# Third mixer of a three-block transformer kernel: latent products as whole jobs before the gate products, head norms regrouped over the engines, attention groups spaced out over the gate blocks

## The reference, cut to what matters

```python
proj = h @ w_in                      # q_lat 192, kv_lat 128, k_rope 32, fq/fk/fv 512 each, f_logit 8, g_mla 1024, g_fox 1024
q  = rms_norm(q_lat) @ w_qb          # 8 heads x (64 nope + 32 rope)
kv = rms_norm(kv_lat) @ w_kvb        # 8 heads x (64 nope + 64 value)
# MLA:  heads normed, rope on q and on the shared k_rope, causal softmax attention
# FoX:  fq, fk normed by head; logits + (c[t] - c[s]), c = cumsum(log_sigmoid(f_logit + b_f))
mixed = sigmoid(g_mla + b0) * (y_mla @ w_branch_mla) + sigmoid(g_fox + b1) * (y_fox @ w_branch_fox)
x = x + mixed @ w_o
```

## Time and profile before

| what | value |
|---|---|
| time, median of 3 runs | 1527.27 us (1527.05 to 1529.64) |
| profiled execution, its own time | 1527.37 us |
| its span | 1525.6 us |
| PE busy | 1489.3 us (98%) |
| DVE, ACT, POOL busy | 876.5, 713.4, 84.6 us |
| mixer three | about 1146.6 to 1334 us of the span |

### The profile page before, as it was taken

How to read it: one execution, slowest core, us unless ns; L and a number is a source line. 1 busy time by engine, 2 the same in 40 slices (tenths; PEclk the granted TensorE clock), 3 DMA queues, 4 the chain that set the end, 5 groups by cost and what they waited for, 6 DMA issues and landing times.

```text
span 1525.6 us, 17528 instructions
## 1 busy us (share of the span) xinstructions
PE 1489.3 (98%) x7341; PEld 1251.1 (82%) x7341; DVE 876.5 (57%) x1051; ACT 713.4 (47%) x846; POOL 84.6 (6%) x101
## 2 busy tenths in 40 slices
PE   8999999999999999999799999999999889999999
PEld 6888888888888888888688888888888768888887
DVE  5464456555445654559765554754547786765453
ACT  6444345544344443344554444543436656454342
POOL 0000012000000000006000000000000440000000
PEclk9999999999999999999999999999999989999999
DMA  8546473455466554644455466554656352555462
GB/s 312 174 146 212 136 257 101 140 181 191 138 217 197 193 182 149 207 147 152 136 180 193 135 210 206 181 192 140 218 169 208 119 166 83 193 177 188 141 225 69
DMA packets 143077, 265.71 MB, mean 174 GB/s; under 512 B 7022, under 2 KB 23878, under 8 KB 142742
## 3 DMA queue, kind: packets, MB, share of 16 engines
q1 hardware_dynamic: 141894, 260.23, 52.0%
q0 software_dynamic: 1104, 4.35, 0.8%
...
...
## 4 chain that ended last, share of the span: by engine, by line
PE 88%; DVE 8%; ACT 2%; POOL 1%; issue 1%; DMA 0%; POOLq 0%; SPq 0%; DVEq 0%; ACTq 0%
PE ps L531 27%; PE ps L533 27%; PE ps L532 27%; DVE wlo L1446 2%; PE ps L560 2%; PE ps L543 1%; ACT whi L1071 1%; PE ps L908 1%; POOL m_qf L2064 0%; PE ps L712 0%; PE ps L656 0%; DVE d_i L1773 0%; DVE X L1501 0%; PE ps L622 0%; DVE d_m L1769 0%
## 5 line engine op out<-in xcount | busy, mean ns | idle before, releaser
L1446 DVE TENSOR_TENSOR wlo<-raw,whi 128x2048 fp32r<-128x2048 f32 (+4 forms) x280 | 570.6, 2042 | 456.4 <-ACT whi L1071 455.4
L1071 ACT CAST whi<-raw 128x2048 fp32r<-128x2048 f32 (+4 forms) x280 | 475.5, 1701 | 484.8 <-PE ps L533 477.1
L531 PE MATMUL ps<-whi,xt_hi 128*128 128x512 f32 (+3 forms) x1472 | 553.3, 376 | 5.6 <-DVE xt_lo L1460 3.0
L533 PE MATMUL ps<-whi,xt_lo 128*128 128x512 f32 (+3 forms) x1472 | 546.8, 371 | 0.0
L532 PE MATMUL ps<-wlo,xt_hi 128*128 128x512 f32 (+3 forms) x1472 | 546.4, 371 | 0.0
L531 PEld LDWEIGHTS ps<-whi,xt_hi 128*128 128x128 f32 x1472 | 278.3, 189 | 55.4 <-DVE xt_lo L1460 4.7
L533 PEld LDWEIGHTS ps<-whi,xt_lo 128*128 128x128 f32 x1472 | 278.2, 189 | 48.0
L532 PEld LDWEIGHTS ps<-wlo,xt_hi 128*128 128x128 f32 x1472 | 278.4, 189 | 45.5
L1093 ACT ACTIVATE junk<-X 128x512 f32<-128x512 f32 x40 | 25.3, 632 | 58.5 <-DVE X L1501 55.0
L531 PE MATMUL ps<-whi,yt_hi 128*128 128x512 f32 (+3 forms) x108 | 43.4, 402 | 8.1 <-DVE wlo L1446 6.9
L533 PE MATMUL ps<-whi,yt_lo 128*128 128x512 f32 (+3 forms) x108 | 42.0, 389 | 0.0
...
## 6 DMA issues: line engine op xcount, KB each, us to landing
...
```

What stands on the lines that cost most here:

```text
L531: e.matmul(o, h, hi_w, start=i == 0 and j == 0, stop=False)
L533: t = e.matmul(o, l, hi_w, start=False, stop=end and j == nk - 1)
L1071: e.copy(whi[0:n, v % SPLIT, c], raw[0:n, v % RAW, c]).then_inc(s_hi.mark(*[(v, j) for j in js]), 1)
L1446: e.tensor_tensor(wlo[0:n, v % SPLIT, c], raw[0:n, v % RAW, c], whi[0:n, v % SPLIT, c].bitcast(F32), ALU.subtract).then_inc(s_lo.mark(*[(v ...
```

## The change

Both parts of w_qb become one job of one block with 768 columns, whose product fills two PSUM pairs, and both halves of w_kvb one job with 1024 columns (block 9). The plan of the mixer is then 26 blocks: 7 is w_qb, 8 fv, 9 w_kvb, 10 to 17 the gates. Both latent products come before the first gate block. The norms of fq and fk share one computation of factors, and POOL multiplies both; DVE multiplies q; the key's rope moves from DVE to POOL. POOL's 16 decay operations become two of 16x256 and two of 16x2048. The second copy of each transposed softmax (P1) moves from DVE to ACT (`flips`). The steps of the two attention kinds are spread over the gate blocks in a new order on PE, ACT and DVE. The diff, indentation cut, lines of removed order left out where the printed functions show them:

```diff
@@ Job, plan, buffers
+self.parts = [(name if c == 0 else f"{name}_{c}", c, min(512, self.width - c)) for c in range(0, self.width, 512)]
...
                                + [(1896 + 512 * i, 512) for i in range(4)], XT, ("xt", "c1"))
-qb = [Job(f"qb{i}", T["mla_w_qb_2"][0], [(0, 2, (128, 64))], [c], YT, ("yt", "lat")) for i, c in enumerate([(0, 512), (512, 256)])]
-kvb = [Job(f"kvb{i}", T["mla_w_kvb_2"][0], [(0, 1, 128)], [(512 * i, 512)], YT, ("yt", "lat"), 2) for i in range(2)]
+qb = Job("qb", T["mla_w_qb_2"][0], [(0, 2, (128, 64))], [(0, 768)], YT, ("yt", "lat"))
...
-    + together(lat, fq) + both(fk) + [(fv, 0), (qb[0], 0), (fv, 1), (qb[1], 0)]
-    + [(gate2[0], 0), (kvb[0], 0), (gate2[0], 1), (kvb[1], 0)] + both(gate2[1]) + both(gate2[2]) + both(gate2[3])
+    + together(lat, fq) + both(fk) + [(fv, 0), (qb, 0), (fv, 1), (kvb, 0)]
+    + both(gate2[0]) + both(gate2[1]) + both(gate2[2]) + both(gate2[3])
...
+r24f = sb("m_rf", [128, 32], F32, sc)
...
-kr_room = [sb("m_kr1", [128, 32], F32, sc), sb("m_kr2", [128, 32], F32, sc)]
...
+kr_room = [mat.P1[:, 0, 0:32], mat.P1[:, 0, 32:64]]
...
@@ TensorE: steps()
+        for pair, (part, c0, w) in zip(pairs, job.parts):
+            hi_w, lo_w = (b[0:n, v % SPLIT, j * wd + c0:j * wd + c0 + w] for b in (whi, wlo))
+            o = pair.ap[:, tt, 0:w]
+            e.matmul(o, h, hi_w, start=i == 0 and j == 0, stop=False)
+            e.matmul(o, h, lo_w, start=False, stop=False)
+            t = e.matmul(o, l, hi_w, start=False, stop=end and j == nk - 1)
+            if j == nk - 1:
+                t.then_inc(s_mm.mark(*([(part, tt)] if end else []), *([(v, tt)] if c0 + w == wd else [])), 1)
...
@@ TensorE: mla()
     def fox_turn(g):
-        q.wait_ge(*s_pool["hn", "fq"])
+        q.wait_ge(*s_pool["hn", "fk"])
...
-        q.wait_ge(*s_dve["hn", "fk"])
...
+    steps(qb, 0)
+    give(qb.parts[0][0], s_act["qf"])
+    give(qb.parts[1][0], s_act["qf"])
     steps(fv, 1)
     give(fv.name, s_act["fv"])
...
+    steps(kvb, 0)
+    give(kvb.parts[0][0], s_act["kv"])
+    give(kvb.parts[1][0], s_act["kv"])
     fox_turn(0)
...
+    steps(gate2[0], 0, 0, 2)
+    fox_scores(0)
+    steps(gate2[0], 0, 2)
     fox_turn(1)
...
+    steps(gate2[0], 1, 0, 2)
     fox_scores(1)
...
+    steps(gate2[0], 1, 2)
+    give(gate2[0].name, s_dve["gate", 0])
+    steps(gate2[1], 0, 0, 2)
     probabilities(mat, ("f", 0), 0)
...
+    steps(gate2[1], 0, 2)
     fox_values(0)
...
+    rope_key_turn()
+    steps(gate2[1], 1, 0, 1)
+    mla_turn(0)
+    steps(gate2[1], 1, 1, 3)
+    mla_scores(0)
+    steps(gate2[1], 1, 3)
+    give(gate2[1].name, s_dve["gate", 1])
     probabilities(mat, ("f", 1), 1)
...
+    steps(gate2[2], 0, 0, 1)
+    mla_turn(1)
+    steps(gate2[2], 0, 1, 3)
     fox_values(1)
...
+    mla_scores(1)
     steps(gate2[2], 0, 3)
...
+    steps(gate2[2], 1, 0, 3)
+    probabilities(mat, ("m", 0), 0)
+    steps(gate2[2], 1, 3)
     give(gate2[2].name, s_dve["gate", 2])
...
+    steps(gate2[3], 0, 0, 1)
     mla_values(0)
+    steps(gate2[3], 0, 1)
     probabilities(mat, ("m", 1), 1)
...
+    steps(gate2[3], 1, 0, 2)
+    mla_values(1)
+    steps(gate2[3], 1, 2)
     give(gate2[3].name, s_dve["gate", 3])
...
@@ ScalarE: mla()
+    def second_copy(g):
+        e.copy(mat.P1[:, :, :], Pair(("m_", "p", g, 1)).flat[:, 0:512].rearrange("p (h t) -> p h t", h=4)).then_inc(s_act.mark(("m_", "P1", g)), 1)
+
+    def flips(g, before=None):
+        probabilities(mat, g, before)
+        q.wait_ge(*s_turn["m_", "p", g, 1])
+        second_copy(g)
...
                          accum_out=s24[:, 2 * i + tt:2 * i + tt + 1]).then_inc(s_act.mark(("latsq", tt, i)), 1)
     unit()
+    norm_squares("fq")
     turned("latt", YT, 0, lambda i: gain(("ql", "ql2", "kvl")[i]), (128, 64, 128))
     unit()
-    norm_squares("fq")
     scaled("fk", lambda tt: FK[:, tt, :], fk, RS)
+    norm_squares("fk")
     unit()
...
+    for part, c0, w in qb.parts:
+        q.wait_ge(*s_mm[part, 1])
+        for tt in range(2):
+            t = e.mul(QF[:, tt, c0:c0 + w], Pair(part).ap[:, tt, 0:w], r_lat[:, tt:tt + 1])
+    t.then_inc(s_act.mark("qf"), 1)
+    unit()
+    norm_squares("q")
     scaled("fv", lambda tt: FV[:, tt, :], fv, RS)
     unit()
+    for part, c0, w in kvb.parts:
+        q.wait_ge(*s_mm[part, 1])
+        for tt in range(2):
+            t = e.mul(KVF[:, tt, c0:c0 + w], Pair(part).ap[:, tt, 0:w], r_lat[:, 2 + tt:3 + tt])
+    t.then_inc(s_act.mark("kv"), 1)
     fox_turn(0)
...
+    norm_squares("k")
     unit()
     fox_turn(1)
+    unit()
     softmax(mat, ("f", 0), 0)
+    unit()
     softmax(mat, ("f", 1), 1)
...
+    flips(("f", 0))
     turned(("m_", "v", ("f", 0)), YT, 4, None, (128,) * 2)
...
     q.wait_ge(*s_turn["m_", "s", ("f", 1), 0])
     q.wait_ge(*s_turn["krt"])
     e.copy(mKT[64:96, :, :], bc(Pair("krt").ap[64:96, 0, 0:256], 1, 8)).then_inc(s_act.mark("krt"), 1)
+    unit()
     mla_turn(0)
+    flips(("f", 1), ("f", 0))
+    unit()
     mla_turn(1)
     softmax(mat, ("m", 0), 0)
+    turned(("m_", "v", ("f", 1)), YT, 6, None, (128,) * 2)
+    unit()
     softmax(mat, ("m", 1), 1)
...
+    flips(("m", 0), ("f", 1))
     unit()
     turned(("m_", "v", ("m", 0)), YT, 0, None, (128,) * 2)
...
+    flips(("m", 1), ("m", 0))
+    unit()
...
@@ VectorE: mla()
...
+    def norm_sums(name, c0):
+        for i, x in enumerate(norm_views[name]):
             n = x.shape[2]
             src = norm_room[i % 2][:, 0:8 * n].rearrange("p (h n) -> p h n", h=8)
             q.wait_ge(*s_act["hnsq", name, i])
             q.wait_ge(*norm_done[0])
...
+            e.tensor_reduce(s24[:, c0 + 8 * i:c0 + 8 * i + 8], src, AX, ALU.add).then_inc(s_dve.mark(("hns", name, i)), 1)
+
+    def norm_factors(names, dst, widths):
         after_mine()
...
+        k = 8 * len(widths)
+        rsqrt(s24, k, [(8 * i, 8, 1.0 / n) for i, n in enumerate(widths)], dst[:, 0:k], ("hnr", names))
...
+    unit()
     q.wait_ge(*s_act["latsq", 1, 2])
     rsqrt(s24, 6, [(0, 2, 1.0 / 192), (2, 2, 1.0 / 128), (4, 2, 1.0 / 32)], r_lat[:, :], ("rs", "lat"))
...
+    norm_sums("fq", 0)
     turned("latt", ("yt", "lat"), YT, 0, lambda i: gain(("ql", "ql2", "kvl")[i]), (128, 64, 128))
     q.wait_ge(*s_turn["ft"])
     e.tensor_scalar(C[64:80, 0, :], Pair("ft").ap[64:80, 1, 0:256], G[64:80, gcols["bff"]:gcols["bff"] + 1], None,
                     ALU.add).then_inc(s_dve.mark("fz"), 1)
     unit()
...
+    after_mine()
+    e.scalar_tensor_tensor(C[64:80, 1, :], C[64:80, 0, :], -1.0, C[64:80, 0, :], ALU.mult, ALU.max).then_inc(s_dve.mark("fabs"), 1)
+    after_mine()
+    e.tensor_scalar(C[64:80, 0, :], C[64:80, 0, :], 0.0, 1.0, ALU.min, ALU.mult).then_inc(s_dve.mark(), 1)
+    norm_sums("fk", 16)
+    norm_factors("f", r24f, (64,) * 4)
+    unit()
+    q.wait_ge(*s_act["fln"])
+    after_mine()
+    e.scalar_tensor_tensor(C[64:80, 0, :], C[64:80, 1, :], -1.0, C[64:80, 0, :], ALU.mult, ALU.add).then_inc(s_dve.mark(), 1)
     q.wait_ge(*s_pool["c_ones"])
     after_mine()
     e.tensor_tensor_scan(C[64:80, 1, :], C[64:80, 2, :], C[64:80, 0, :], 0.0, ALU.mult, ALU.add).then_inc(s_dve.mark("c"), 1)
...
+    unit()
+    unit()
+    norm_sums("q", 0)
+    norm_factors("q", r24, (64, 64, 32, 32))
+    after_mine()
+    for i, x in enumerate(norm_views["q"]):
+        e.tensor_tensor(x, x, r24[:, 8 * i:8 * i + 8].unsqueeze(2).broadcast_to([128, 8, x.shape[2]]),
+                        ALU.mult).then_inc(s_dve.mark(*([("hn", "q")] if i == 3 else [])), 1)
+    unit()
+    norm_sums("k", 0)
+    norm_factors("k", r24, (64, 64))
     unit()
     logits(mat, ("f", 0), 0, 1.0, causal)
+    unit()
+    normalise(mat, ("f", 0), 0)
     logits(mat, ("f", 1), 1, 1.0, causal, ("fxk", 1))
...
+    unit()
+    gate(0)
     normalise(mat, ("f", 1), 1)
...
     turned(("m_", "v", ("f", 0)), ("yt", "fox"), YT, 4, None, (128,) * 2)
...
+    unit()
+    logits(mat, ("m", 0), 0, 96.0 ** -0.5, causal, ("m_", "p", ("f", 0), 1))
+    unit()
+    gate(1)
+    normalise(mat, ("m", 0), 0)
     turned(("m_", "v", ("f", 1)), ("yt", "fox"), YT, 6, None, (128,) * 2)
...
     logits(mat, ("m", 1), 1, 96.0 ** -0.5, causal, ("m_", "p", ("f", 1), 1))
...
+    unit()
     normalise(mat, ("m", 1), 1)
     unit()
     gate(2)
...
     turned(("m_", "v", ("m", 0)), ("yt", "mla"), YT, 0, None, (128,) * 2)
...
+    unit()
+    turned(("m_", "v", ("m", 1)), ("yt", "mla"), YT, 2, None, (128,) * 2)
     gate(3)
     unit()
...
@@ GpSimd: mla()
...
+    def scale_heads(names, rows_):
+        views = [v for n in names for v in norm_views[n]]
         for i, x in enumerate(views):
             after_mine()
...
+            t = e.tensor_tensor(x, x, rows_[:, 8 * i:8 * i + 8].unsqueeze(2).broadcast_to([128, 8, x.shape[2]]), ALU.mult)
+            t.then_inc(s_pool.mark(*([("hn", names[-1])] if i == len(views) - 1 else [])), 1)
+
+    q.wait_ge(*s_dve["rs", "lat"])
+    q.wait_ge(*s_gate["all"])
+    for tt in range(2):
+        kr = KR[:, tt, 64:96]
+        after_mine()
```

(77 more changed lines are left out.)

97 lines of the change are left out of this document (7 added, 90 removed).

## The result

The changed kernel takes 1534.35 us, median of 6 runs (1533.26 to 1536.39); the kernel before, run beside it, 1529.61 (1527.05 to 1530.4). The ratio is 1.0036, interval [1.0023, 1.0049]: slower, by some 3.5 to 7.5 us. The profiled spans say the same, 1531.5 against 1525.6 us. The forecast was slower, 1539.

The account below looks back on a forecast made before the run. PE was taken as the bound. Waits of 24.8 us against 11.8 gave +13.0, clock 0, small gaps -1.0: net +12.0 on the profiled execution's 1527.4, so 1539 us, range 1522 to 1546.

Parts of the forecast that it names:

- the two large waits: PE waits 10.4 us in the keys' half of fox_turn(1), for DVE's logits, and 5.4 in mla_turn(1), for gate(1).
- the clock's cost: PE's slow spells behind waits: 5.6 us behind the gaps of 10.4 and 5.4, against 5.7 before, so 0 net.
- Step 1: Block 8 on DVE: PE, done with w_qb, waits 1.7 us for its split.
- Step 5: Pair of gate 1: PE waits 5.4 us in mla_turn(1), as gate(1) on DVE stands behind the split of block 16.
- The small waits: fox_values(0) and mla_scores(0) wait some 0.4 us each for ACT, 0.8 in the sum.
- faster: Rival, chance 0.10: with short holds, the pair in mla_turn(1) is also read in time; 1519 us.
- Short holds: Rival, chance 0.17: POOL's long additions hold DVE only briefly, the 10.4 us wait in fox_turn(1) goes; 1529 us.
- step 4: DVE held up to 9.2 us by POOL's two additions; first FoX logits late, PE waits 10.4 us in fox_turn(1).
- Steps 2 and 3: PE waits 3.1 us at gate 0 for ACT's kv scaling, then 3.4 at the FoX scores for POOL's decay rows.
- the 1.0 us: Small gaps at PE's switches between products and transposes, estimated to vanish in the waits: -1.0 us in the sum.

Follow-up runs that it names:

- gate first: Changed kernel with gate(1) moved ahead of the split of block 16 on DVE; 1527.86 us, ratio 1.0003 to the kernel before.
- rows cut: Changed kernel with POOL's two 16x2048 additions cut to one head of eight, the other rows zero; 1532.03 us, ratio 1.0023 to the kernel before.
- small rows: Changed kernel with the 16 decay operations of 16x256 of before back on POOL; 1534.77 us, ratio 1.0043 to the kernel before.
- logits first: Changed kernel with the first FoX logits on DVE directly behind block 11, before block 12 and the k norm; 1532.7 us, ratio 1.0029.
- both: Changed kernel with gate(1) before block 16 and the first FoX logits before the k norm; 1526.48 us, ratio 0.9989 to the kernel before.
- late key norm: As both, with the k norm behind the second logits and gate(0), first normalisation behind the second logits; 1522.91 us (0.9970), again 1523.6 (0.9974).
- Block 8 first: Changed kernel with the split of block 8 ahead of the shared factors of fq and fk on DVE; 1535.38 us, ratio 1.0058.
- four rooms: Changed kernel with four work buffers instead of two for ACT's squares of the head norms; 1534.4 us, ratio 1.0050 to the kernel before.

## Why the prediction was right, and where it was too high

**Right.** PE's work and busy time unchanged; DVE the late engine; the two large waits in the two places and with the two releasers named; the clock's cost the same as before (mixer busy 125.9 in both). Step 1: 1.5 us for 1.7. Step 5: 5.2 for 5.4, and gate first shows that its mechanism is the one given, the gate behind the split of block 16. The small waits: 0.8 for 0.8. The *faster* rival needed `gate(1)` within 1.8 us of the probabilities, and it ended at 1260.8, 6.5 us behind the end of their last transposes. *Short holds* falls as well: holds of 2.2 and 3.3 us can be read directly, and rows cut has their price.

**Too high by 6 us on the profiled execution, 4.7 by the median; first term: step 4, the size of additions and holds.** I had bounded an addition between 4.2 and 5.2 us, and it took 3.60, below the lower bound. The holds were put at the full length of both, 9.2 us; they were 5.5. Of these 3.7 us, 2.0 are the additions' own length, and most of the rest comes from the first one, which had begun 1.25 us before DVE came to an operation that it holds. From the q factors to their last instruction DVE took 8.7 us where the sum had 13.3, and although it began them 1.2 late, the logits began at 1220.8 and not at 1224.4. That is 3.6 us of the 6.

**Second term: where the clock's cost lies.** Behind the two large waits I had 5.6 us. Behind the first, PE's starts from 1222.05 to 1226.22 lose 1.9 us against the same instructions at the full clock, behind the second 1.4, together 3.3. The rest of the low clock, 2.7 us from 1190 to 1197, came ahead of the logits, where PE would have waited anyway. By both corrections the sum is 12.0 - 3.6 - 2.3 = 6.1; the mixer time says 6.2. That they meet to 0.1 us is luck: the 1.0 us below, which the sum had taken off, is not in this reckoning, and step 5's 0.2 neither.

**Steps 2 and 3: two single waits wrong, without effect.** The ring's wait was 1.5 (forecast 3.1), and there was none for the decay rows (3.4). The ring's was short by the clock: gate 0 began 32.3 us after the first mark in the changed kernel as in rows cut, small rows, logits first, gate first, both and late key norm, where the wait is 2.7 us, near the forecast; in the changed kernel the longer spell at the lower clock (from 1189.3 to 1195.4) filled 1.2 of them. Both waits stand ahead of the logits on PE, while DVE sets when those come: had they been right, the 9.0 us would have been smaller by as much. Block 8 first and four rooms confirm it. The rows had a margin of 0.6 us (ready at 1206.05, scores at 1206.64), and small rows turned it into a wait of 2.7. The 1.0 us that I let vanish in the gaps at each switch did not vanish: idle time is 17.96 us, all of it in the table of waits.

**Still open.** What decides whether PE runs at the lower clock behind a wait, and for how long. The same instructions behind nearly the same wait do both. Behind the 5.2 us before `mla_turn(1)` the transposes of the keys took 1.53 us in the changed kernel and 1.91 in rows cut, and there six products followed at the low clock. Behind the 1.5 us for block 8, the 512-column products are slow from the start in the changed kernel and until 1195.4; in gate first, whose programs are the same up to there, seven are (0.63 us each), and in four rooms none is:

```profile
1189.26 0.79 PE L534 MATMUL ps<-whi,xt_hi 128*128 128x512 f32 x1 [1.48 <-DVE wlo L1458]
```

```profile
1189.88 0.50 PE L534 MATMUL ps<-whi,xt_hi 128*128 128x512 f32 x1 [1.47 <-DVE wlo L1458]
...
1190.72 0.63 PE L534 MATMUL ps<-whi,xt_hi 128*128 128x512 f32 x1
```

```profile
1188.86 0.50 PE L535 MATMUL ps<-whi,xt_hi 128*128 128x512 f32 x1 [1.47 <-DVE wlo L1457]
...
1205.80 1.97 PE L626 MATMUL ps<-m_kt,m_qt 80*128 80x256 f32 x8 [2.72 <-POOL m_kt L2088]
```

So a part of every mixer time in the table, 1 to 3 us, can be clock that the edit does not explain; the readings above rest on waits, or on larger differences. No run was made that holds the waits and changes only what stands ahead of them.
